# Issuing the first three gathers of expert rows in the router's block, and copying the first unit's early chunks in another order

## The reference

```python
def moe_ffn(h, router_w, router_b, w_gate_up, b_gate_up, w_down, b_down):
    ...
    logits = (xt @ router_w + router_b).astype(jnp.float32)
    top_v, top_i = lax.top_k(logits, TOP_K)
    gates = jax.nn.softmax(top_v, axis=-1)
    ...
    def expert_block(args):
        idx, e = args
        xb = xpad[idx]
        gu = xb @ w_gate_up[e] + b_gate_up[e]
        x_glu = jnp.minimum(gu[:, ::2], SWIGLU_LIMIT)
        x_lin = jnp.clip(gu[:, 1::2], -SWIGLU_LIMIT, SWIGLU_LIMIT)
        act = x_glu * jax.nn.sigmoid(SWIGLU_ALPHA * x_glu) * (x_lin + 1.0)
        return act @ w_down[e] + b_down[e]
```

## Time and profile before

| | us |
|---|---|
| median of 3 runs | 1849.71 (1849.27 to 1853.72) |
| profiled execution, its own time | 1849.57 |
| its span, first to last instruction | 1848.0 |
| PE busy | 1646.6 (89%) |
| DVE busy | 1188.8 (64%) |
| ACT busy | 980.4 (53%) |
| experts' block, about | 368 to 1432 |

### The profile page before, as it was taken

How to read it: one execution, slowest core, us unless ns; L and a number is a source line. 1 busy time by engine, 2 the same in 40 slices (tenths; PEclk the granted TensorE clock), 3 DMA queues, 4 the chain that set the end, 5 groups by cost and what they waited for, 6 DMA issues and landing times. The chain is left out here.

```text
span 1848.0 us, 54844 instructions
## 1 busy us (share of the span) xinstructions
PE 1646.6 (89%) x16925; PEld 869.4 (47%) x16926; DVE 1188.8 (64%) x2018; ACT 980.4 (53%) x1772; POOL 404.2 (22%) x467
## 2 busy tenths in 40 slices
PE   6999889769899999989987999999886469998897
PEld 3999754424333333323332333333231146877753
DVE  4785443657677777757764677777653275963665
ACT  5334532157577777757764677677553244534412
POOL 0000000023233333323322233333221300630000
PEclk9999989879999999989999999999997679999999
DMA  9872574095989999996699999999999722221101
GB/s 339 262 248 92 165 185 174 32 405 230 424 338 388 421 424 424 424 424 263 268 424 425 425 424 407 423 424 415 424 424 398 291 74 69 80 58 49 57 5 46
DMA packets 136741, 520.87 MB, mean 282 GB/s; under 512 B 20163, under 2 KB 59092, under 8 KB 87381
## 3 DMA queue, kind: packets, MB, share of 16 engines
q1 hardware_dynamic: 118132, 487.87, 66.5%
q0 software_dynamic: 18240, 31.46, 4.7%
q10 hardware_dynamic: 290, 0.48, 0.1%
HBM read 494.73 MB, written 24.91 MB: 281 GB/s over the span
## 5 line engine op out<-in xcount | busy, mean ns | idle before, releaser
L1888 DVE COPY ring<-staging 128x1024 f32 (+1 forms) x956 | 646.8, 695 | 306.6 <-SPq L1646 119.1
L1811 ACT ACTIVATE ring<-staging 128x512 f32 (+1 forms) x956 | 589.8, 631 | 348.1 <-PE banks L1753 131.9
L1753 PE MATMUL banks<-staging,rowsT 128*32 (+1 forms) x1268 | 591.6, 614 | 71.6 <-DVE ring L1888 66.2
L1753 PE MATMUL banks<-ring,rowsT 128*32 128x512 f32 x3840 | 600.9, 615 | 0.0
L1753 PEld LDWEIGHTS banks<-staging,rowsT 128*32 128x32 f32 x1268 | 125.9, 110 | 467.0 <-issue 448.8
L1776 PE MATMUL banks<-staging,hiddenT 128*32 x1280 | 298.9, 385 | 2.3 <-DVE ring L1888 1.1
L1776 PE MATMUL banks<-ring,hiddenT 128*32 128x256 f32 x3840 | 300.4, 386 | 0.0
L1776 PEld LDWEIGHTS banks<-staging,hiddenT 128*32 128x32 f32 x1280 | 132.8, 111 | 173.9 <-issue 92.4
L1694 POOL COPY rows_leaving<-y_rows 128x256 f32<-128x256 f32 x80 | 46.6, 582 | 497.0 <-ACT y_rows L1834 493.0
L606 PE MATMUL banks<-w_in_hi,hT 128*128 128x256 f32 (+1 forms) x768 | 147.1, 291 | 1.1 <-issue 1.1
L1776 PEld LDWEIGHTS banks<-ring,hiddenT 128*32 128x32 f32 x3840 | 147.7, 111 | 0.0
(11 more groups left out here) (437 smaller groups left out, 2020.2 us busy)
## 6 DMA issues: line engine op xcount, KB each, us to landing
staging<-in_w_gate_up SPq DMA_DIRECT2D x250, 1024.0 KB, 12.5
staging<-in_w_down SPq DMA_DIRECT2D x128, 1024.0 KB, 12.7
stage<-in_w_mod SPq DMA_DIRECT2D x21, 1024.0 KB, 6.1
stage<-in_w_in SPq DMA_DIRECT2D x25, 512.0 KB, 4.0
stage<-in_w_in SPq DMA_DIRECT2D x11, 1024.0 KB, 5.6
expert_rows<-rows_leaving POOLq DMA_DIRECT2D x80, 128.0 KB
expert_rows<-catT SPq DMA_DIRECT2D x1, 7936.0 KB
early<-in_w_gate_up SPq DMA_DIRECT2D x6, 1024.0 KB
```

The lines of the kernel that those rows point to most:

```text
L1753: mm = pe.matmul(k.bank(0)[c * SLOTS:(c + 1) * SLOTS, :], rowsT[:, q % 2, row], w, start=first and q == 0, stop=not first and q == KT - 1, ...
L1811: act.activation(ring[:, pos % RING, BY_ACT], staged(i, e, pos, 3 * PART, PART), ACT.Copy).then_inc(act_filled, 1)
L1888: dve.tensor_copy(ring[:, pos % RING, BY_DVE], staged(i, e, pos, PART, 2 * PART)).then_inc(dve_filled, 1)
```

## The change

The gathers of units 0, 1 and 2 move from the experts' block into the router's, to POOL, which has nothing else to do there. For that `slot`, the three buffers and their semaphores are made earlier, and DVE writes the first column of `k.slots` by itself, ahead of the other 511, and `k.table` ahead of `k.lane`. In the experts' block, chunks 6 and 7 of unit 0 are filled ahead of all copies of early chunks; these copies are given out anew (DVE 0 and 1 ahead of `pick_expert(1)` and `linear(0)`, 3 and 4 behind `finish_hidden(0)`; ACT 2 ahead of `gate(0)`, 5 behind `rows_turned(1)`); and PE waits for them only ahead of unit 1.

```diff
+def gather_rows(k, pool, i, code, out, at, done):
+    pool.tensor_copy(k.slot[:, at:at + 1], k.slots[:, code]).then_inc(k.slot_ready, 1)
+    pool.wait_ge(k.slot_ready, i + 1)
+    pool.sem_inc(k.slot_seen, 1)
+    pool.indirect_dma_start(
+        out=out[:], out_offset=None, in_=k.d["h2"].rearrange("t (c n) -> (t c) n", c=QUARTERS),
+        in_offset=bass.IndirectOffsetOnAxis(ap=k.slot[:, at:at + 1], axis=0)).then_inc(done, 16)
...
+            @block.gpsimd
+            def _(pool):
+                pool.wait_ge(h2_out, 16 * NT)
+                pool.wait_ge(slots_ready, 1)
+                gather_rows(k, pool, 0, slice(0, 1), k.first_rows[0], 1, k.first_in[0])
+                pool.wait_ge(slots_ready, 2)
+                pool.wait_ge(table_ready, 1)
+                gather_rows(k, pool, 1, bass.ds(code_of(k, pool, 1), 1), k.first_rows[1], 2, k.first_in[1])
+                gather_rows(k, pool, 2, bass.ds(code_of(k, pool, 2), 1), k.first_rows[2], 0, k.rows_in)
...
-                dve.tensor_scalar(k.slots[:], k.bank(2)[:, 0:CODES], float(QUARTERS), token[:, NT:NT + 1], ALU.mult,
-                                  ALU.add)
+                for part in (slice(0, 1), slice(1, CODES)):
+                    dve.tensor_scalar(k.slots[:, part], k.bank(2)[:, part], float(QUARTERS), token[:, NT:NT + 1],
+                                      ALU.mult, ALU.add).then_inc(slots_ready, 1)
                 dve.wait_ge(plan_ps, 1)
+                dve.tensor_copy(k.table[:, 0:2 * P], k.bank(5)[0:1, 0:2 * P]).then_inc(table_ready, 1)
                 dve.tensor_copy(k.lane[:], k.bank(5)[:, 2 * P:3 * P])
-                dve.tensor_copy(k.table[:, 0:2 * P], k.bank(5)[0:1, 0:2 * P])
...
-                gather(0, y, 1, first_in[0])
-                gather(1, rows, 2, first_in[1])
-                gather(2, landing, 0, rows_in)
                 for m in range(2):
                     pool.wait_ge(first_in[m], 16)
                     pool.sem_inc(rows_here, 1)
...
-                pe.wait_ge(settled, EARLY)
                 turn_hidden(0)
                 turn_rows(2)
                 add_bias(1)
+                pe.wait_ge(settled, EARLY)
...
-                for pos in range(RING - 1, 6):
+                for pos in range(RING - 1, KT):
                     fill(0, 0, pos)
-                for m in (1, 3, 5):
-                    act.wait_ge(chunk_done, m + 1)
-                    act.activation(own_slot(m), k.early_slab(m), ACT.Copy).then_inc(settled, 1)
-                fill(0, 0, 6)
-                fill(0, 0, 7)
                 act.wait_ge(act_filled, KT)
                 act.sem_inc(act_filled, CHUNKS - KT)
+                settle(2)
                 gate(0)
                 rows_turned(1, KT)
+                settle(5)
                 act.wait_ge(settled, EARLY)
...
-                for pos in range(RING - 1, 6):
+                for pos in range(RING - 1, KT):
                     fill(0, 0, pos)
-                for m in (0, 2, 4):
-                    dve.wait_ge(chunk_done, m + 1)
-                    dve.tensor_copy(own_slot(m), k.early_slab(m)).then_inc(settled, 1)
-                fill(0, 0, 6)
-                fill(0, 0, 7)
-                pick_expert(1)
                 dve.wait_ge(dve_filled, KT)
                 dve.sem_inc(dve_filled, CHUNKS - KT)
+                settle(0)
+                settle(1)
+                pick_expert(1)
                 linear(0)
                 finish_hidden(0)
+                settle(3)
+                settle(4)
                 e_next = expert_on(dve, 1)
```

More of the change, by code:

```diff
@@ L231, in routing, with code_of @@
     k.table = k.sb("table", [1, TABLE], I32, at=scope)
+    k.slot = k.sb("slot", [P, LINE], I32, at=scope)
+    k.first_rows = [k.sb(f"rows{m}", [P, D // QUARTERS], at=scope) for m in range(3)]
+    k.first_in = [k.sem(f"first_rows{m}_in") for m in range(2)]
+    k.rows_in = k.sem("rows_in")
+    k.slot_ready = k.sem("slot_ready")
+    k.slot_seen = k.sem("slot_seen")
+def gather_rows(k, pool, i, code, out, at, done):
[5 more added lines that the diff above has]
+        in_offset=bass.IndirectOffsetOnAxis(ap=k.slot[:, at:at + 1], axis=0)).then_inc(done, 16)
+def code_of(k, pool, i):
+    return pool.value_load(k.table[0:1, bass.ds(i + P, 1)], min_val=0, max_val=CODES - 1)
 def early_weights(k, weights):
@@ L1250, in stage_router @@
         plan_ps = sem("plan_ps")
+        slots_ready = sem("slots_ready")
+        table_ready = sem("table_ready")
         rank_bank = lambda t: k.bank((1, 3)[t % 2])
@@ L1553, in stage_experts @@
         pick = sb("pick", [P, P], F32R)
-        slot = sb("slot", [P, LINE], I32)
-        landing = sb("rows_landing", [P, D // QUARTERS])
-        rows = sb("rows", [P, D // QUARTERS])
+        y, rows, landing = k.first_rows
         rowsT = sb("rowsT", [P, 2, P])
@@ L1560, in stage_experts @@
         hT = sb("hiddenT", [P, 2, P])
-        y = sb("y_rows", [P, D // QUARTERS])
         leaving = sb("rows_leaving", [P, D // QUARTERS])
@@ L1573, in stage_experts @@
         pick_used = sem("pick_used")
[L1574 to L1577, removed]
+        rows_in, first_in = k.rows_in, k.first_in
         rows_here = sem("rows_here")
@@ L1670, in _, with gather @@
                 units = units_on(pool)
[L1671 to L1680, removed]
+                def gather(i):
+                    gather_rows(k, pool, i, bass.ds(code_of(k, pool, i), 1), landing, 0, rows_in)
                 def move_rows(i):
@@ L1705, in _ @@
                 move_rows(2)
-                gather(3, landing, 0, rows_in)
+                gather(3)
                 pool.sem_inc(y_free, 1)
                 move_rows(3)
-                gather(4, landing, 0, rows_in)
+                gather(4)
                 store_rows(0)
@@ L1712, in _ @@
                     move_rows(i + 2)
-                    gather(i + 3, landing, 0, rows_in)
+                    gather(i + 3)
                     store_rows(i - 1)
@@ L1834, in read_y, with settle @@
                     act.activation(y[:], k.bank(4)[:, 0:GLU], ACT.Copy).then_inc(y_read, 1)
+                def settle(m):
+                    act.wait_ge(chunk_done, m + 1)
+                    act.activation(own_slot(m), k.early_slab(m), ACT.Copy).then_inc(settled, 1)
                 rows_turned(0, 0)
@@ L1910, in pick_expert, with settle @@
                                       ).then_inc(pick_ready, 1)
+                def settle(m):
+                    dve.wait_ge(chunk_done, m + 1)
+                    dve.tensor_copy(own_slot(m), k.early_slab(m)).then_inc(settled, 1)
                 for pos in range(RING - 1):
```

## The result

The changed kernel takes 1863.78 us (median of 6 runs, 1859.97 to 1864.21), the kernel before beside it 1853.3 us (6 runs, 1849.27 to 1855.94). The ratio is 1.0057, with a 95% interval from 1.0044 to 1.007: slower by 0.6%, some 10 us, where a gain of 5.5 us was forecast. The profiled execution took 1859.97 us, with a span of 1858.4 us.

The account below looks back on a forecast made before the run. The bound was taken to alternate between DMA at its ceiling and PE, passing on unit 1's start one for one: 6.5 us earlier less 1.0 for PE's clock, 5.5 off 1849.57, gave 1844.1 us, range 1840 to 1850.

Parts of the forecast that it names:

- What bounds the kernel: Experts' block: the bound alternates between DMA at some 424 GB/s and PE, linked by ring releases at 436 and 893.
- DMA at its ceiling: Experts' block behind the release at 436: loads run at some 424 GB/s, so an earlier unit 1 shifts the end one for one.
- the one on the other side of no change: Rival, experts' block: weight loads from chunk 6 on come 5.35 us later and decide, 1855.0 us; chance 0.07 with other losses.
- another loss: Any loss other than the later weight loads, no place or size given; shares the chance of 0.07 with them.
- The gathers and the barrier: Router's end: POOL ends its gathers at 372.7, last at the barrier; SP starts at 373.5, 5.35 us later than before.
- the 0.37 us that were left out of the sum: First gather, moved into the router: takes 0.37 us less without DVE's copies beside it; time would be 0.4 us lower.
- the block's end holds POOL until its last gather has landed: Worst case at the router's end: POOL held until 379.0 in place of 372.7, costs 6.3 us, leaves 1850.4 us.
- Unit 0 to unit 1: Front of the experts' block: `linear` 8.7 us earlier, two DVE copies behind `finish_hidden`, unit 1 at 392.9, 6.5 us earlier.
- PE's clock: Start of unit 1: half clock expected at 392.9, rising 3 to 6 us later; 1.0 us taken off the gain.
- The sum: Whole kernel: 6.5 us at unit 1 less 1.0 for the clock, a gain of 5.5 us, to 1844.1 us.
- if SP starts after 375: Sign that the prediction is wrong: SP's first issue of the experts' block after 375, where near 373.5 was forecast.
- Gone at 500 or 900: Sign that the prediction is wrong: the 5 us are there at 430 and gone at 500 or 900 in the experts' block.

Follow-up runs that it names:

- pad128: The kernel before with an unused buffer of 128 bytes per partition ahead of the weights; 1862.06 us, ratio 1.0047.
- pad64: The kernel before with an unused buffer of 64 bytes per partition ahead of the weights; 1866.9 us, ratio 1.0072.
- pad_behind: The kernel before with 64 unused bytes per partition behind the ring of weights, which stays at byte 9728; 1851.66 us, ratio 0.9995.
- changed_aligned: The changed kernel with `slot` in an unused part of `eps`, so the weights start at byte 12800, a multiple of 512; 1847.88 us, ratio 0.9968.
- wait_landed: changed_aligned with POOL also waiting at the end of the router's block until all three gathers have landed; 1848.08 us (1 run).
- one_gather: changed_aligned with only unit 0's gather in the router's block, those of units 1 and 2 back in the experts' block; 1844.69 us, ratio 0.9951.
- order_only: The kernel before with only the change's order of fills and copies, gathers still in the experts' block; 1849.46 us, ratio 0.9985.
- interleaved: one_gather with each early chunk copied in parts right ahead of its fill, by the engine that reads it, PE's part by ACT; 1842.01 us, ratio 0.9938.
- copies_first: The kernel before with chunks 0 to 5 copied to their own places at the block's start, where unit 0 reads them; 1846.01 us, ratio 0.9965.

## Why the prediction was wrong

**What bounds the kernel**: right. The block alternates as described; SP's long waits are still there (26.08 us of issue time around the first).

**The step that failed**: "DMA at its ceiling", the link by which every gain at the front was passed on "one for one". The ceiling was taken over from the rows of before as if it held whatever the edit did. It depended on where the kernel puts its weights. With the loads' place 128 bytes off a multiple of 512 it fell from 422 to 415 GB/s, and 983 us behind chunk 24 became 998. No rival named it: the one on the other side of no change was a delay of the early loads (1855.0), and the measured time lies beyond that too; "another loss" shared its chance of 0.07 and had no mechanism. The section on the change said that the buffers are made earlier, in another scope, and the prediction costed that edit at nothing without a look at addresses. pad128, pad64, pad_behind and changed_aligned show this cause, in both directions. It accounts for 15.3 us (998.35 - 983.09) behind chunk 24, and by the ratios for 1.0057 - 0.9968 = 0.89%, some 16 us.

**The gathers and the barrier**: the mechanism right, the size off. SP was to start 5.35 us later and started 7.1 us later (9.68 - 2.54). The gathers themselves took 6.07 us (363.91 to 369.98) against 6.39 before, so of the 0.37 us that were left out of the sum 0.32 came; but the crossing behind POOL took 2.8 us and not 0.83. The bound "the block's end holds POOL until its last gather has landed" had, as far as wait_landed tells, the right mechanism in view with too long a landing: 7.3 us behind the gather's start, where the bytes of wait_landed had moved 2.5 us behind it (371.45 to about 374).

**Unit 0 to unit 1**: right. Without the copies in its way `linear` came early, two DVE copies stood behind the hidden rows, and unit 1 gained 5.1 us of the 6.5. Unit 0 started 1.4 us earlier in place of 3.2, short by the barrier's 1.8, and the stretch from there to unit 1 was 3.8 us shorter (15.80 against 19.58) where 3.3 were forecast.

**PE's clock**: the direction right. I took 1.0 us; from unit 1 to chunk 24 the changed kernel took 39.76 us, before 37.76 and 38.65 in its two traces: 1.1 to 2.0 us. pad64, with the old order, took 39.31, so part of that may be chance too. Unit 1 began at half clock, as feared:

```profile
391.50:396.00 4.50, 4.28 (x22) 1.04 (x26) 2.18 (x5) 2.49 (x6) 1.81 (x3) 0.50 1.01 422
397.00:401.00 4.00, 4.00 (x40) 1.01 (x32) 2.99 (x5) 2.90 (x5) 0.00 (x0) 1.00 1.00 408
```

**The sum**: with the weights on a multiple of 512 it was 0.9968 [0.9956, 0.998], a gain of 3.7 to 8.1 us, which holds the 5.5 forecast. But the terms don't hold: the barrier cost 1.8 us more than its term. By the marks the gain is less: chunk 24 at 69.18 behind the plan against 71.52 and 72.72, 2.3 to 3.5 us. Which is nearer stays open; so the agreement with 5.5 may be luck.

**The signs that were named**: chunk 23 went out at 404.87 + 26.08 - 0.33 = 430.6, where 430.8 was forecast. That is luck: 2.5 us of it are the router's earlier end. The sign "if SP starts after 375" seems not to have come (372.78), but counted behind the plan it did: 9.68 us behind 365.63 would be 375.3. "Gone at 500 or 900" came true, the lead going from 5.7 us at 431 to nothing near 770. It was set down as a sign and had no mechanism behind it.

**What stays open.** Why the address matters. The starts tried are 9728 and 12800 (423 to 424 GB/s from 600 to 800), and 9792, 9856 and 12928 (415, 418 and 416). All the good ones are multiples of 512 and so of 256 too, so the runs don't say which it takes; nor were `early` and `staging` moved apart. The Trainium skill ("DMA: Bandwidth & Descriptors", section "How a descriptor splits into AXI transactions") says that a descriptor that doesn't start on a 256-byte boundary costs extra beats of 32 bytes, and says it of reads. Applied to a written packet of 8192 bytes, it would be an estimated 2 beats in 256 for 64 bytes and 4 for 128, 0.8% and 1.6%. Measured are 1.9% for 64, and 1.2% (pad128) and 1.7% (the changed kernel) for 128: of that order of size, but not smaller for 64, so I hold it for a hint and no explanation. A kernel without the copies of the early chunks, which write to the bytes that they read, wasn't run.

## What to carry to other kernels

An edit that adds a buffer moves every buffer made behind it. Before a buffer is costed at nothing, compare the start of each large DMA target before and after; and where all DMA-bound stretches of a trace are lower by the same per cent, look there first, and pad to the old alignment as a test. A bound that a gain is passed through must be shown to be untouched by the edit: here the front was worth 2 to 9 us and the rate of the long plateau behind it 15. And count marks from the last event ahead of the edit: the router's end alone moved by up to 4.4 us from trace to trace.

To start work ahead of a barrier, move only what is needed first: one gather gave all that three gave and cost 4 us less. And put small copies where PE waits anyway, not between two dense stretches, where PE's clock is lost as well. Before that, look at the addresses of a copy's two ends: here they were the same.

## What the runs showed of the hardware

- Starting 64 or 128 bytes past a multiple of 512 slowed the weight loads to SBUF by 1.2% to 1.9% (423 to 418 and 415 GB/s), with the DMA engines' share as full as ever; a packet of 8192 bytes took 315 to 317 ns in place of 310 to 311. Moving what lies behind the target by 64 bytes cost nothing (0.9995). Starts 256 bytes past a multiple of 512 weren't tried.
- Where the end of a block stood behind an indirect DMA of GpSimd, SP's first issue came 2.6 to 2.8 us behind that instruction's end (one_gather 2.64, the changed kernel 2.80), against 0.83 us behind a DVE write.
- With copies between the two units, PE had 1.13 busy us of the 4 from 390 to 394 and the granted clock was 0.50 in the 4 behind (order_only). Where no copies stood there, PE had 2.28 and 2.41 busy us in the same window, the clock stayed at 1.00 (interleaved, copies_first), and the work from unit 1 to chunk 24 took 37.1 us in place of 39.5 to 40.0.
